# Routing of the expert layer from unscaled, transposed x, in plain 32 bit

## The reference, cut to what matters

```python
def moe_ffn(h, router_w, router_b, w_gate, w_up, w_down):   # h = rmsnorm_2(x, g)
    t = h.reshape(b * s, d)                                  # 256 x 1024
    logits = (t @ router_w) + router_b                       # 256 x 8
    top_vals, top_idx = lax.top_k(logits, TOP_K)             # 2 of 8
    top_w = jax.nn.softmax(top_vals, axis=-1)
    gates = jnp.sum(jax.nn.one_hot(top_idx, N_EXPERTS) * top_w[..., None], axis=1)
    for e in range(N_EXPERTS):
        out = out + gates[:, e:e + 1] * swiglu_2(t, w_gate[e], w_up[e], w_down[e])
```

## Time and profile before

| | us |
|---|---|
| median of 3 runs | 2785.78 |
| lowest and highest run | 2784.59, 2790.94 |
| the profiled execution's own time | 2793.5 |
| span of that execution | 2790.5 |
| PE busy | 2661.5 (95%) |
| PEld busy | 2271.1 (81%) |
| DVE busy | 2003.0 (72%) |
| ACT busy | 1476.8 (53%) |
| transfers, mean rate over the span | 216 GB/s |

### The profile page before, as it was taken

The page is one execution under the profiler, slowest core; times in us unless marked ns, Lnnn a source line. Parts: engine busy times, 40 slices in busy tenths (PEclk is TensorE's granted clock), DMA queues, the critical chain, the costliest instruction groups (busy, mean ns, idle before and its releaser), DMA issues.

```text
span 2790.5 us, 46467 instructions
## 1 busy us (share of the span) xinstructions
PE 2661.5 (95%) x18240; PEld 2271.1 (81%) x18240; DVE 2003.0 (72%) x1864; ACT 1476.8 (53%) x1436; POOL 87.9 (3%) x82
## 2 busy tenths in 40 slices
PE   8999998999999989999999887999999999999997
PEld 7888897888888888888889886787777878787876
DVE  6665776666665866667666654888788878888886
ACT  4444424444444504455446623676666667666665
POOL 6000005000000000000000000000000000000000
PEclk9999999999999999999999998999999999999999
DMA  8564313555663314565565305999999989998992
GB/s 278 195 198 132 105 49 106 185 192 180 193 190 121 97 33 151 185 200 168 187 192 143 129 2 182 342 347 346 314 340 343 347 316 345 340 347 326 331 349 104
DMA packets 343041, 602.01 MB, mean 216 GB/s; under 512 B 12000, under 2 KB 180832, under 8 KB 342752
## 3 DMA queue, kind: packets, MB, share of 16 engines
q1 hardware_dynamic: 335264, 590.85, 62.3%
q10 hardware_dynamic: 7616, 8.85, 1.0%
HBM read 598.61 MB, written 1.05 MB: 215 GB/s over the span
## 4 chain that ended last, share of the span: by engine, by line
PE 55%; DMA 28%; DVE 8%; ACT 5%; DVEq 2%; issue 2%; another core or an unknown queue 1%; ACTq 0%; PEldq 0%; SPq 0%; PEld 0%; POOLq 0%
DMA raw<-in_ffn_w_down 20%; PE ps L2791 14%; PE ps L2820 8%; PE ps L2795 7%; PE ps L971 5%; DVE wlo L314 4%; PE ps L2825 4%; DMA raw<-in_dn_w_in 3%; ACT whi L310 3%; DMA raw<-in_w_in 2%; PE ps L589 1%; PE ps L2844 1%; PE ps L2832 1%; PE ps L1339 1%; DMA raw<-in_pool_w_in 1%
## 5 line engine op out<-in xcount | busy, mean ns | idle before, releaser
L314 DVE TENSOR_TENSOR wlo<-raw,whi 128x2048 fp32r<-128x2048 f32 (+1 forms) x394 | 902.3, 2290 | 202.3 <-ACT whi L310 194.2
L310 ACT CAST whi<-raw 128x2048 fp32r<-128x2048 f32 (+1 forms) x394 | 751.3, 1909 | 312.6 <-DMA raw<-in_ffn_w_down 142.7
L2791 PE MATMUL ps<-whi,xboth 128*128 128x512 f32 x1792 | 462.7, 400 | 5.4 <-remote 2.9
L565 PE MATMUL ps<-xboth,whi 128*128 128x512 f32 x1680 | 420.8, 392 | 0.0
L2791 PEld LDWEIGHTS ps<-whi,xboth 128*128 128x128 f32 x1792 | 332.6, 189 | 81.6 <-issue 16.2
L565 PEld LDWEIGHTS ps<-xboth,whi 128*128 128x128 f32 x1680 | 305.3, 189 | 57.2
L314 DVE TENSOR_TENSOR wlo<-U,whi 128x2048 fp32r<-128x2048 f32 x112 | 256.4, 2289 | 70.9 <-ACT whi L310 68.1
L310 ACT CAST whi<-U 128x2048 fp32r<-128x2048 f32 x112 | 213.9, 1910 | 92.8 <-DMA U<-in_moe_w_up 79.9
L2795 PE MATMUL ps<-wlo,xboth 128*128 128x512 f32 x896 | 241.6, 391 | 6.6 <-issue 6.6
L568 PEld LDWEIGHTS ps<-xboth,wlo 128*128 128x128 f32 x1680 | 229.2, 190 | 16.4
L568 PE MATMUL ps<-xboth,wlo 128*128 128x256 f32 x1680 | 234.2, 282 | 0.0
(11 more groups left out here) (525 smaller groups left out, 3647.4 us busy)
## 6 DMA issues: line engine op xcount, KB each, us to landing
raw<-in_moe_w_gate SPq DMA_DIRECT2D x58, 1024.0 KB, 5.7
raw<-in_moe_w_up SPq DMA_DIRECT2D x56, 1024.0 KB, 5.9
U<-in_moe_w_up SPq DMA_DIRECT2D x56, 1024.0 KB, 6.4
U<-in_moe_w_down SPq DMA_DIRECT2D x56, 1024.0 KB, 5.2
raw<-in_ffn_w_gate SPq DMA_DIRECT2D x55, 1024.0 KB, 5.4
raw<-in_ffn_w_up SPq DMA_DIRECT2D x55, 1024.0 KB, 5.3
raw<-in_ffn_w_down SPq DMA_DIRECT2D x55, 1024.0 KB, 4.9
work<-in_moe_w_gate SPq DMA_DIRECT2D x54, 1024.0 KB, 6.1
```

The source lines that it names most:

```text
L310: act.copy(whi[:, n % SPLIT, 0:width], buf[:, 0:width]).then_inc(hi_ready[n % RAW], 1)
L314: dve.tensor_tensor(wlo[:, n % SPLIT, 0:width], buf[:, 0:width], whi[:, n % SPLIT, 0:width], ALU.subtract).then_inc(split_ready[n % SPLIT], 1)
L565: pe.matmul(ps[:, first_bank + b, :], whi[:, n % SPLIT, c * GW + b * P:c * GW + (b + 1) * P], xboth[:, c].rearrange("p a t -> p (a t)"), s ...
L2791: pe.matmul(dst, part[:, k * C // 2 + c, xhalf(q)], whi[:, (m + k) % SPLIT, c * EW:(c + 1) * EW], start=(k == 0 and c == 0 and part is xhi ...
```

## The change

1. `route_tensor` transposes x as it is, each quarter on its `x_part`, against the identity (four transposes of 128x128, into banks 4 to 7). ACT copies the first two turned quarters to SBUF between its squares, DVE the last two (`turned_part`).
2. The router's weights are multiplied by g once (`nar_gain`, 128x64). The logits are formed token-major: 8 products a token tile, turned x stationary and 8 columns moving, in plain 32 bit. The norm's factor is multiplied in with the bias, by one DVE instruction a token tile.
3. `moe_x` is x times the norm's factor only, made by ACT. The weight g is applied behind the gather: `gather_hi` and `gather_lo` are four instructions of 128x128 each instead of one of 128x512, at the entry and in the loop. The row copy `moe_row` and its load go.
4. At the entry of `moe` the two halves of the gather are handed on one by one, and the first gate tile needs the first only.
5. ACT's `refill_scalar` (the split of a weight tile) moves behind the exponential. `mean_ahead` is off for `dn_out`.

```diff
+turned_tok = [v.rearrange("p (c t) -> p c t", c=C) for v in (ye, work[:, 512:1536])]
+nar_gain = nar[:, C * E:2 * C * E]
+moe_gain = second_vec("norm_ffn_g_2", C)
+moe_gains = vec[:, DEPTH * NLV + SV["norm_ffn_g_2"] + C:DEPTH * NLV + SV["norm_ffn_g_2"] + 2 * C]
...
-    norm_tensor(pe, FFN_BANK)
-    for c in range(C):
-        wait_xt(pe, c)
-    narrow_tensor(pe, 8)
-    narrow_turn_tensor(pe, 8)
+    for i, (t, s) in enumerate(PARTS):
+        pe.wait_ge(f["x_part"], i + 1)
+        for c in range(4 * s, 4 * s + 4):
+            tr = pe.transpose(ps[:, 4 + i, (c % 4) * P:(c % 4 + 1) * P], x[:, t, c * P:(c + 1) * P], const("ident"))
+        tr.then_inc(f["transposed"], 1)
+    for t in range(TT):
+        if t == 0:
+            take(pe, f["turned_act"], 2)
+            pe.wait_ge(f["narrow_lo"], 1)
+        else:
+            take(pe, f["xt_ready"], 2)
+        for c in range(C):
+            mm = pe.matmul(ps[:, 2 + t, 0:E], turned_tok[t][:, c, :],
+                           nar_gain[:, c * E:(c + 1) * E], start=(c == 0), stop=(c == C - 1))
+        mm.then_inc(f["narrow_done"], 1)
...
-    act.dma_start(moe_row, a["norm_ffn_g_2"][1, :].partition_broadcast(P)).then_inc(f["vecs"], 16)
...
+def turned_part(i):
+    t, s = PARTS[i]
+    return turned_tok[t][:, 4 * s:4 * s + 4, :], four(4 + i)
...
-    norm_scalar(act, second_vec("norm_ffn_g_2", C), FFN_BANK, moe_scratch)
+    act.activation(tiny[:, 72:73], small("one"), ACT.Sqrt)
+    for i, (t, s) in enumerate(PARTS):
+        act.wait_ge(f["x_part"], i + 1)
+        act.activation(moe_scratch, x_half(t, s), ACT.Square, scale=1.0 / 32, accum_out=tiny[:, i:i + 1])
+        act.drain().then_inc(f["sq_part"], 1)
+        if i < 2:
+            act.wait_ge(f["transposed"], i + 1)
+            act.copy(*turned_part(i)).then_inc(f["turned_act"], 1)
+    for t in range(TT):
+        act.wait_ge(f["mean"], t + 1)
+        act.activation(tiny[:, 10 + t:11 + t], tiny[:, 4 + t:5 + t], ACT.Sqrt).then_inc(f["root"], 1)
+    act.sem_clear(f["mean"])
+    for t in range(TT):
+        act.wait_ge(f["scaled"], t + 1)
+        act.activation(moe_x[:, t, :], x[:, t, :], ACT.Copy, scale=tiny[:, 6 + t:7 + t]).then_inc(f["moe_x"], 1)
+    act.sem_clear(f["scaled"])
     act.dma_start(final_row, a["final_norm_g_2"].partition_broadcast(P)).then_inc(f["grow_in"], 16)
-    dn_norm_small_scalar(act, None, E)
-    refill_scalar(act, n)
     act.wait_ge(f["top"], 1)
     act.activation(wts[:, :, 0:1], wts[:, :, 1:2], ACT.Exp).then_inc(f["top_exp"], 1)
+    refill_scalar(act, n)
     return n
...
-    norm_vector(dve, second_vec("norm_ffn_g_2", C), FFN_BANK)
-    narrow_vector(dve, E)
-    dve.wait_ge(f["vecs"], 32)
-    for t in range(TT):
-        dve.scalar_tensor_tensor(out=moe_x[:, t, :], in0=x[:, t, :], scalar=tiny[:, 6 + t:7 + t], in1=moe_row,
-                                 op0=ALU.mult, op1=ALU.mult)
-    narrow_row_vector(dve, E)
+    dve.wait_ge(f["narrow_in"], 16)
+    dve.tensor_tensor(nar_gain.rearrange("p (c e) -> p c e", c=C), nar[:, 0:C * E].rearrange("p (c e) -> p c e", c=C),
+                      moe_gains.unsqueeze(2).to_broadcast([P, C, E]), ALU.mult).then_inc(f["narrow_lo"], 1)
+    dve.wait_ge(f["transposed"], 3)
+    dve.tensor_copy(*turned_part(2)).then_inc(f["xt_ready"], 1)
+    mean_vector(dve, 0)
+    dve.wait_ge(f["transposed"], 4)
+    dve.tensor_copy(*turned_part(3)).then_inc(f["xt_ready"], 1)
+    for t in range(TT):
+        rstd_vector(dve, t)
+        dve.sem_inc(f["scaled"], 1)
+    dve.sem_clear(f["transposed"])
...
-    dve.wait_ge(f["narrow_done"], 1)
-    dve.tensor_tensor(logit, ps[:, 6, 0:16].rearrange("p (t e) -> p t e", t=TT),
-                      bias_r.unsqueeze(1).to_broadcast([P, TT, E]), ALU.add)
+    dve.wait_ge(f["vecs"], 16)
+    for t in range(TT):
+        dve.wait_ge(f["narrow_done"], t + 1)
+        dve.scalar_tensor_tensor(out=logit[:, t, :], in0=ps[:, 2 + t, 0:E], scalar=tiny[:, 6 + t:7 + t],
+                                 in1=bias_r, op0=ALU.mult, op1=ALU.add)
...
     take(pe, f["picked"])
+    pe.wait_ge(f["moe_x"], TT)
     for b in range(2):
-        mm = gather(2 + b, b)
-    mm.then_inc(f["gathered"], 1)
-    take(pe, f["xt_ready"])
-    gate(n, 0, 0)
+        gather(2 + b, b).then_inc(f["gathered"], 1)
+
+    def first_rows(k):
+        pe.wait_ge(f["xt_ready"], k + 1)
+        if k == 1:
+            pe.sem_clear(f["xt_ready"])
+    by_token(n, ps[:, 4, :], 0, first_rows)
...
     def gather_hi(bank, b, q):
-        return act.copy(xhi[:, 4 * b:4 * b + 4, xhalf(q)], four(bank))
+        for c in range(4 * b, 4 * b + 4):
+            hi = act.activation(xhi[:, c, xhalf(q)], four(bank)[:, c % 4, :], ACT.Copy, scale=moe_gain(c))
+        return hi
...
-    take(act, f["gathered"])
     for b in range(2):
-        hi = gather_hi(2 + b, b, 0)
-    hi.then_inc(f["gather_hi"], 1)
+        act.wait_ge(f["gathered"], b + 1)
+        gather_hi(2 + b, b, 0).then_inc(f["gather_hi"], 1)
+    act.sem_clear(f["gathered"])
...
     def gather_lo(bank, b, q):
-        return dve.tensor_tensor(xlo[:, 4 * b:4 * b + 4, xhalf(q)], four(bank), xhi[:, 4 * b:4 * b + 4, xhalf(q)],
-                                 ALU.subtract)
+        for c in range(4 * b, 4 * b + 4):
+            lo = dve.scalar_tensor_tensor(out=xlo[:, c, xhalf(q)], in0=four(bank)[:, c % 4, :], scalar=moe_gain(c),
+                                          in1=xhi[:, c, xhalf(q)], op0=ALU.mult, op1=ALU.subtract)
+        return lo
...
-    take(dve, f["gather_hi"])
     for b in range(2):
-        lo = gather_lo(2 + b, b, 0)
-    lo.then_inc(f["xt_ready"], 1)
+        dve.wait_ge(f["gather_hi"], b + 1)
+        gather_lo(2 + b, b, 0).then_inc(f["xt_ready"], 1)
+    dve.sem_clear(f["gather_hi"])
...
-add_out("dn_out", "dn_w_out_2", lambda l: 0, route_loads, True, open_far)
...
```

7 lines of the change are left out of this document (4 added, 3 removed).

## The result

| | before | changed |
|---|---|---|
| median of 5 runs on the same chip, us | 2787.83 | 2773.34 |
| lowest and highest, us | 2784.59, 2790.94 | 2767.65, 2776.06 |
| the profiled execution's own time, us | 2793.5 | 2776.06 |
| its span, us | 2790.5 | 2774.2 |

The ratio of the times is 0.9945, with a 95% interval of 0.9930 to 0.9961: 15 us faster, 11 to 20. The forecast was 2775 us, in a range of 2768 to 2782.

The account below looks back on a forecast made before the run. PE sets the pace in the loop; ahead of it a chain of short steps is in the open. Gains of 7.2 + 2.2 + 1.7 = 11.1 us off 2785.8 gave 2774.7, rounded 2775, range 2768 to 2782.

Parts of the forecast that it names:

- Step 1: Entry, first square to the search of the best two: search starts at 1708.2 instead of 1716.1, 7.9 us earlier.
- PE is hidden under this: Entry: PE's transposes and logit products end before the norm's factor is ready; at worst logits come 0.8 us later.
- Step 2: Entry, behind the search: ACT's exponential comes late for DVE, 0.7 us lost, so the gather starts 7.2 us earlier.
- The ranks: Entry, from the exponential to the use of the ranks: 1.46 us, nearly all DVE's own small instructions.
- Step 3: Hand-over of the gather: gate tile starts 7.3 us behind the gathers instead of 9.5, 2.2 us gained.
- Step 4: First gate tile: runs at the upper clock level after only 0.7 us of PE idle time, 1.7 us gained.
- The loop: Four instructions for one on ACT and DVE, 14 times: hidden, nothing lost; without cover up to 17 us.
- its signs: Loop costs would show as longer groups g = 5 and 6, or new PE idle time before L2833 or down products.
- the named cover: Loop: ACT's 0.81 us idle ahead of the second cast and DVE's 1.87 us in the group behind hide the added instructions.
- only the start is carried: Rival: the transfer stream is the bound, only its 7.2 us earlier restart reaches the end: 2778.6 us; chance 11%.
- The lower clock: Rival: the first gate tile still runs at the lower clock level, 9.4 us gained, 2776.4 us; chance 17%.

Follow-up runs that it names:

- e4_busy: Changed kernel plus PE products of a zero tile in PE's idle times up to the gathers, and 12 counting instructions: 2770.84 us, ratio 0.9939 to before.
- e5_whole: Changed kernel, but the first gate tile waits for both gathered halves, plus 52 counting instructions on PE: 2773.99 us, ratio 0.9958 to before.
- e6_one: Changed kernel with one instruction for four at both ends of a gathered half, weights g left out there, 51 counting instructions: 2771.53 us, ratio 0.9950 to before.
- e7_order: Changed kernel with DVE's third weight tile subtraction and two memsets moved behind the gathered halves, 50 counting instructions: 2766.86 us, ratio 0.9935 to before.

## Why the prediction was right, and where not

The time was right, the sum behind it was not: 8.5 us of the 11.1 came true, and a place it did not look at gave most of the rest. That the median fell on the forecast to 2 us is luck. The range was not: with the 8.5 us alone, less what is lost behind the last Silu (1.4 in this pair), the prediction's own sum gives 2785.8 - 7.1 = 2778.7, an estimate that still lies in it.

**Step 1, up to the search: 7.9 forecast, 5.9 measured.** ACT's and DVE's lists were right: their single steps came up to 0.3 us earlier than worked out, and DVE was ready at 1707.93 (1707.9). The failed sentence is "PE is hidden under this", with 0.8 us as the upper bound of its cost. Each product in plain 32 bit is two records in the trace. I divided the 6.61 us of the gather by its 32 records and took 0.21 us as the upper price of a product; by the code these are 16 products (8 a half, not the 16 a half that the description of the kernel has), 0.41 us each. The two lots of logits took 5.5 us instead of 3.3, the second of them, at 1.2 GHz, 3.56 for its 8 products. e4_busy separates the two parts: at full clock the search starts at 6.98 us, so 1.7 of the 2.0 us are the clock, and 0.3 the rest. The upper bound of 0.8 us for this term was thus too low.

**Step 2, the exponential: 0.7 us lost forecast, 0 measured.** With the search 2.0 us later the load found room. In e4_busy, where the search was as early as 6.98 us, the function followed the load at once, in ACT's timeline:

```profile
1707.12 1.28 ACT L2667 ACT_TABLE_LOAD   x1
1708.41 0.21 ACT L2667 ACTIVATE work<-work 128x2 f32<-128x2 f32 x1
```

That is 8.76 us behind the first square, where 9.1 was forecast, and DVE's next instruction on it was 2.02 us behind the search, 0.1 later than before. So even with an early search the loss is 0.1. The Trainium skill ("ScalarE: Activation LUTs", "What ACT_TABLE_LOAD costs") has another 1.38 us of drain; the rows do not show it: the load starts 0.03 us behind the end of ACT's instruction ahead of it, and the function 1.29 us behind the start of the load, as in the trace of before.

**The ranks: 1.46 us to their use "nearly all DVE's own".** That sentence missed PE's five products between. At 1.2 GHz they took 2.3 instead of 1.3 us, and DVE waited 1.13 us for them. In e4_busy the 1.0 us was gone. The gathers thus started 4.9 us earlier (7.2 forecast).

**Step 3, the hand-over: 2.2 forecast, 2.2 measured** (9.51 to 7.35 us). Handing the halves on singly is 1.15 of it (e5_whole); DVE's four instructions took 1.14 us (1.2 forecast), and one instead would be 0.4 us shorter (e6_one). That DVE's own list is what the first half waits for is shown by e4_busy, where PE's faster gathers changed nothing, and by e7_order.

**Step 4, the clock of the first gate tile: 1.7 forecast, 1.5 measured.** The tile ran at the upper level. The reason given, a short idle time (0.7 us forecast, 1.70 measured), is not enough: see e5_whole.

**The loop: nothing forecast, nothing measured** for four for one in the loop itself, by the equal groups of e6_one; the last item, behind it, is open: group 49, with its second half, is 1.6 us longer than before, and PE has new idle time before L2833 (1.02 us), which the prediction had named as its signs. DVE's stop of 2.91 us stands in that group, and e6_one does not separate the two. ACT's idle time before its second cast fell from 0.81 us to 0.60, so the named cover was used and held.

**Not foreseen: the jumps.** Groups 15 and 29 gave 8.7 us in the two traces. The stop of 3.45 us stood in the trace of before, in the loop of which the windows said that PE is full, and the 140 us window that I read ended before the first jump. The Trainium skill ("Runtime: NRT & Kernel Launch", "Instruction fetch mechanics") says that instructions are fetched in pieces of 16 KiB (256 instructions) and that a taken branch out of the loaded pieces forces a fetch before execution goes on. The rows agree on the pieces for PE's queue (16,384 bytes); they differ on the stop: PE went on 0.8 to 0.9 us behind the jump and stood later. Nor were the stops of ACT and DVE behind the loop foreseen; they cancel in this pair (135.2 and 135.4 us), by luck as far as is known.

Of the rivals, "only the start is carried" is refuted: what the entry gained, 8.5 us and not 4.9, was still there in full at the first jump. The lower clock came true, but at logits and ranks instead of the gate tile, and for the same reason that e4_busy shows: PE had been idle between short lots.

## What to carry to other kernels

When an edit removes instructions ahead of a hardware loop, look at the jumps in the trace before pricing anything: here a stop labelled "issue" a few products behind the head moved or vanished with the number of instructions in front, and two kernels should be compared with the head at the same place. Such stops exist in the lists of the other engines too: compare group by group, since a sum can hide two differences that cancel. Here a chain of short products on a mostly idle TensorE had to be priced at 1.2 GHz, and a count in a row was a count of records, not of products. Where two engines release the same step, speeding up one shows nothing until the other's list is shortened as well: 0 and 1.1 us apart, 5.5 together at the first Silu.
